# The hi and lo halves of the weights interleaved element by element in one tile: a decoder trunk on one core

## The chip, the cores and the metric

The kernel runs on one core of a Trainium2 chip. The metric is the device time of one execution in microseconds (us). A core has five engines that run beside each other, each with its own queue of instructions and held together by semaphores: TensorE (PE, with its weight loads as PEld), VectorE (DVE), ScalarE (ACT), GpSimdE (POOL) and SyncE (SP), which here issues the DMAs.

## What is computed

The reference is a decoder trunk over 512 tokens of width 1024 with two layers. The first mixes the tokens with a Mamba-2 SSD mixer, the second with differential attention with ALiBi; behind each stands a gated feed-forward net with a causal depthwise convolution of width 3. Every mixer is wrapped in an RMS norm before and one after it. All of it is float32, and most of the arithmetic is in eight matrix products with weights:

```python
proj = jnp.einsum('bsd,de->bse', u, w_in)          # SSD mixer, 1024 -> 6176
return jnp.einsum('bse,ed->bsd', y, w_out)         # 2048 -> 1024
h = jnp.einsum('bsd,df->bsf', u, w_up)             # net, 1024 -> 5632, twice
return jnp.einsum('bsf,fd->bsd', silu(gate) * up, w_down)   # 2816 -> 1024, twice
qkv = jnp.einsum('bsd,de->bse', u, w_qkv)          # attention, 1024 -> 3072
return jnp.einsum('bse,ed->bsd', out, w_out)       # 1024 -> 1024
```

## The kernel before

The activations lie transposed in SBUF, features over the 128 partitions and the 512 tokens along the free dimension, in chunks of 128 features. A product with a weight matrix is made in units: one unit is the weights of 128 output features for 8 chunks of input (1024 columns of 128x128 tiles, 512 KB) or, in the two down projections, for 11 chunks (1408 columns). There are 217 units in eight phases, in this order: MIX (49 units, the input projection of the SSD mixer, in a loop over 8 groups of 6 units with the scan's own matmuls between them), SOUT (16), UP0 (44), DN0 (16), QKV (24, in a loop over the heads with the attention between them), AOUT (8), UP1 (44), DN1 (16).

To keep float32 precision at the single-pass rate of the float32r type, every float32 operand is split into two float32r halves: hi, the rounded value, and lo, the rest. A tile product is then three matmuls: hi x hi and hi x lo with the hi half of the weights, and lo x hi with their lo half. That is `product` (lines 466 to 470): line 468 and 469 take the weights' hi half, line 470 their lo half. Each of the three is a matmul instruction with a weight load of its own, 128 columns in 128 partitions.

Of each unit SyncE loads the float32 weights into the tile `raw` (two slots, line 386). ScalarE copies them into the hi half (`split_hi`, line 416). VectorE subtracts hi from raw and writes the lo half (`split_lo_dve`, line 431); in the attention loop GpSimdE does that for 20 units (`split_lo`, line 422). TensorE then runs the unit. `w_hi` and `w_lo` have two slots each, so ScalarE may write a slot only when TensorE has finished the unit that was in it, two units back. To start a phase early there are further pairs of tiles: `own_hi`/`own_lo`, `fx_*`, `fy_*` for the feed-forward phases, and `ax_*`, `ay_*` for attention; `halves_of` (lines 322 to 333) names the pair of a unit. Hi and lo are two separate tiles in each case, and in each the elements of a unit are contiguous: the 128 weights of one load lie 4 bytes apart.

The moving operands are the activations, split in the same way (`hn_hi`/`hn_lo`, `y_*`, `h_*`, `o_*`), 512 tokens to a matmul in most cases. At the four boundaries between mixer and net the work goes by halves of the tokens, 256 columns to a matmul: the last pair of units of a phase (`pair_pe`, two pairs where the phase has two units to an output) and the first four units of the next one (`wide_start`), so that the norm of the first half of the tokens can run beside the products of the second.

The order on each engine is written out by hand. In VectorE's queue the split of a unit some places ahead stands between the steps of the convolution or of the attention (`ahead`), and ScalarE's splits stand between its activations. The waits around the change are: ScalarE waits in line 416 for the unit that frees its slot (`unit_done`) and for the DMA, VectorE in line 431 for hi (`hi_made`), TensorE at the head of a unit for lo (`lo_made`), and SyncE for lo too, before it loads over the raw slot.

Of the kernel before, what the change touches and what calls it, by code (L numbers as in the profile page):

```python
# [18 lines left out]
F32R = mybir.dt.float32r  # L19
# [4 lines left out]
P = 128  # L24
# [3 lines left out]
KC = D // P  # L28
# [9 lines left out]
UW = HU * P  # L38
# [65 lines left out]
def trunk(nc, x_in, w_mix, w_sout, w_up0, w_dn0, w_qkv, w_aout, w_up1, w_dn1, params, lam_in, out):  # L104
    ctx = ExitStack()
    with ctx:
        MIX, SOUT, UP0, DN0, QKV, AOUT, UP1, DN1 = PH = phases()
# [3 lines left out]
        def sb(name, shape, dt=F32, scope=ctx):  # L111
            return scope.enter_context(nc.sbuf_tensor(name, shape, dt))
# [4 lines left out]
        x = sb("x", [P, KC, S])  # L117
        raw = sb("raw", [P, 2, UW])
        sb("lead_in", [P, 56])
        w_hi = sb("w_hi", [P, 2, UW], F32R)  # L120
        w_lo = sb("w_lo", [P, 2, UW], F32R)
        sb("lead_out", [P, 72])
        par = sb("par", [P, NPAR])
        lam_v = sb("lam_v", [P, 4 * DH])
# [28 lines left out]
        with ExitStack() as ssm:  # L153
# [38 lines left out]
            ecs_bc = sb("ecs_bc", [P, HG, S], scope=ssm)  # L192
            sb("own_lead", [P, 112], scope=ssm)
            own_raw = sb("own_raw", [P, KC * P], scope=ssm)
            own_hi, own_lo = sb("own_hi", [P, KC * P], F32R, scope=ssm), sb("own_lo", [P, KC * P], F32R, scope=ssm)
        with ExitStack() as ffn:
            h_hi = sb("h_hi", [P, FC, S], F32R, scope=ffn)
            h_lo = sb("h_lo", [P, FC, S], F32R, scope=ffn)
            with ExitStack() as lap:
                ug_f = sb("ug_f", [P, FFN_T - 1 + S], scope=lap)  # L200
                cg = sb("cg", [P, S], scope=lap)
                cu = sb("cu", [P, S], scope=lap)
                sg = sb("sg", [P, S], scope=lap)
                hb = sb("hb", [P, S], scope=lap)
            fy_hi, fy_lo = sb("fy_hi", [P, 2, KC * P], F32R, scope=ffn), sb("fy_lo", [P, 2, KC * P], F32R, scope=ffn)
            fx_hi, fx_lo = sb("fx_hi", [P, 2, KC * P], F32R, scope=ffn), sb("fx_lo", [P, 2, KC * P], F32R, scope=ffn)
        with ExitStack() as att:
            o_hi = sb("o_hi", [P, NH, S], F32R, scope=att)
            o_lo = sb("o_lo", [P, NH, S], F32R, scope=att)
            qT = sb("qT", [P, 2, S], scope=att)  # L210
            kT = sb("kT", [P, 2, S], scope=att)
            vT = sb("vT", [P, 2, S], scope=att)
            vtok = sb("vtok", [P, 2, NB, P], scope=att)
            dist_i = sb("dist_i", [P, S], mybir.dt.int32, scope=att)
            dist = sb("dist", [P, S], scope=att)
            sc = sb("sc", [P, 2, 2, S], scope=att)
            pr = sb("pr", [P, 2, 2, S], scope=att)
            at = sb("at", [P, NB, S], scope=att)
            aT = sb("aT", [P, NB, S], scope=att)
            ob = sb("ob", [P, S], scope=att)  # L220
            on = sb("on", [P, S], scope=att)
            with ExitStack() as lap:
                osq = sb("osq", [P, S], scope=lap)
                nmx = sb("nmx", [P, 2, 2], scope=lap)
                den = sb("den", [P, 2, 2], scope=lap)
                cf = sb("cf", [P, 2, 2], scope=lap)
            ay_hi, ay_lo = sb("ay_hi", [P, 2, KC * P], F32R, scope=att), sb("ay_lo", [P, 2, KC * P], F32R, scope=att)
            ax_hi, ax_lo = sb("ax_hi", [P, 2, KC * P], F32R, scope=att), sb("ax_lo", [P, 2, KC * P], F32R, scope=att)

        bank = [ctx.enter_context(nc.psum_tensor(f"bank{i}", [P, S], F32)) for i in range(2)]  # L230
        b_norm = ctx.enter_context(nc.psum_tensor("b_norm", [P, S], F32))
# [84 lines left out]

        WIDE = (UP0, QKV, UP1)

        def slot_of(ph, j):
            return (ph.U0 + j) % 2  # L320

        def halves_of(ph, j, first=False):

            if first and ph in WIDE and j < 4:
                own = ((ax_hi, ax_lo), (ay_hi, ay_lo)) if ph is QKV else ((fx_hi, fx_lo), (fy_hi, fy_lo))
                hi, lo = own[j // 2]
                return hi[:, j % 2, :], lo[:, j % 2, :]
            if first and (ph is MIX and j == 2 or ph is SOUT and j == 6):
                return own_hi[:], own_lo[:]
            if first and ph is AOUT and j in (2, 3):  # L330
                return ax_hi[:, j - 2, 0:ph.width], ax_lo[:, j - 2, 0:ph.width]
            slot = slot_of(ph, j)
            return w_hi[:, slot, 0:ph.width], w_lo[:, slot, 0:ph.width]

        def acc_of(ph, j):
            return bank[(ph.Q0 + j) % 2]
# [14 lines left out]
        def raw_of(ph, j, first=False):  # L351
            if first and ph is MIX and j == 2:
                return own_raw[:]
            return first_raw[:, j, :] if first and ph in WIDE else raw[:, slot_of(ph, j), 0:ph.width]
# [108 lines left out]

        def product(acc, slot, c, hi, lo, first, last, weights=None):

            wh, wl = weights or (w_hi[:, slot, :], w_lo[:, slot, :])
            wh, wl = wh[:, c * P:(c + 1) * P], wl[:, c * P:(c + 1) * P]
            nc.tensor.matmul(acc[:], wh, hi, start=first, stop=False)  # L468
            nc.tensor.matmul(acc[:], wh, lo, start=False, stop=False)  # L469
            return nc.tensor.matmul(acc[:], wl, hi, start=False, stop=last)  # L470
# [1694 lines left out]
```

## Time and profile before

| | us |
|---|---|
| median of 3 runs | 1436.48 (1435.9 to 1438.88) |
| the profiled execution | 1436.27 |
| its span, from the first instruction to the last | 1434.5 |
| TensorE matmuls busy | 1417.3 (99%) |
| weight loads busy | 1192.6 (83%) |
| VectorE busy | 1027.8 (72%) |
| ScalarE busy | 621.3 (43%) |
| GpSimdE busy | 112.9 (8%) |

Busy times are unions of the recorded spans of an engine's instructions. Matmuls are pipelined and their recorded ends are modelled, so that neighbours overlap: the rate of the stream is the distance between two starts, not the recorded duration. In the timeline a row is start, duration, engine, line, operation, what is written and read, and the shapes; a row that merges several instructions ends with their count. L468 is line 468. "bank<-hn_hi,w_hi" is a matmul into the tile bank with hn_hi moving and w_hi as weights; 128x512 is the moving operand with its columns. PEclk is the TensorE clock that was granted, as a share of full speed.

### The profile page before, as it was taken

What the parts mean: (1) busy time and instruction counts of PE and PEld (TensorE: products, weight loads), DVE (VectorE), ACT (ScalarE), POOL (GpSimd) and SP (SyncE); (2) the same over time, 40 slices, a digit from 0 to 9 for tenths busy, and PEclk for the clock granted to TensorE, in tenths of its full rate; (3) what the DMA queues carried; (4) which work ended last, traced back from release to release, by engine and by line L of the source; (5) the groups of instructions that cost most, each with busy time, mean ns of one, the idle gap of its engine ahead of it and who ended that gap; (6) DMA issues with size and microseconds to landing.
All of it is one profiled execution on the core that took longest, in us unless ns stands there. A gap on an engine that the chain in (4) does not pass through costs nothing.

```text
span 1434.5 us, 21763 instructions
## 1 busy us (share of the span) xinstructions
PE 1417.3 (99%) x7506; PEld 1192.6 (83%) x7506; DVE 1027.8 (72%) x1575; ACT 621.3 (43%) x1019; POOL 112.9 (8%) x85
## 2 busy tenths in 40 slices
PE   8999999999999999999999999999999999999997
PEld 6888888888889888888888977777798888888887
DVE  6998889899437888888623677778588888886123
ACT  6656555557334323323323446556563332323221
POOL 0000000000110000000011032321110000000111
PEclk9999999999999999999999999999999999999999
DMA  4433332432231232323233112121212222233331
GB/s 169 176 137 126 142 125 109 138 140 74 89 132 38 96 102 88 102 91 110 101 101 139 31 59 74 59 74 56 89 63 84 92 102 96 94 105 103 101 101 60
DMA packets 37445, 142.34 MB, mean 99 GB/s; under 512 B 4176, under 2 KB 6352, under 8 KB 35344
## 3 DMA queue, kind: packets, MB, share of 16 engines
q1 hardware_dynamic: 37392, 141.63, 28.8%
q8 instruction: 34, 0.56, 0.2%
q14 instruction: 19, 0.16, 0.0%
HBM read 139.38 MB, written 2.23 MB: 99 GB/s over the span
## 4 chain that ended last, share of the span: by engine, by line
PE 94%; DVE 3%; DMA 1%; ACT 1%; issue 1%; SPq 0%; POOL 0%; POOLq 0%; ACTq 0%
PE bank L468 20%; PE bank L470 20%; PE bank L469 20%; PE b_x L468 7%; PE b_x L470 7%; PE b_x L469 7%; PE b_norm L1647 1%; PE b_norm L489 1%; PE b_y L1080 1%; PE b_y L468 1%; PE b_y L470 1%; PE b_y L469 1%; PE b_cb L1607 1%; DVE hn_lo L823 1%; PE b_x L1092 1%; PE b_y L1597 1%
## 5 line engine op out<-in xcount | busy, mean ns | idle before, releaser
L416 ACT ACTIVATE w_hi<-raw 128x1024 fp32r<-128x1024 f32 (+1 forms) x201 | 222.9, 1109 | 406.3 <-PE bank L470 291.1
L431 DVE TENSOR_TENSOR w_lo<-raw,w_hi 128x1024 fp32r<-128x1024 f32 (+1 forms) x181 | 234.1, 1293 | 229.2 <-ACT w_hi L416 229.1
L468 PE MATMUL bank<-hn_hi,w_hi 128*128 128x512 f32 x848 | 335.9, 396 | 2.9 <-DVE hn_lo L804 1.6
L470 PE MATMUL bank<-hn_hi,w_lo 128*128 128x512 f32 x848 | 330.8, 390 | 0.0
L469 PE MATMUL bank<-hn_lo,w_hi 128*128 128x512 f32 x848 | 330.3, 389 | 0.0
L468 PEld LDWEIGHTS bank<-hn_hi,w_hi 128*128 128x128 f32 x848 | 159.3, 188 | 38.1 <-DVE w_lo L431 3.2
L470 PEld LDWEIGHTS bank<-hn_hi,w_lo 128*128 128x128 f32 x848 | 159.2, 188 | 33.9
L469 PEld LDWEIGHTS bank<-hn_lo,w_hi 128*128 128x128 f32 x848 | 159.4, 188 | 32.1
L468 PE MATMUL bank<-h_hi,w_hi 128*128 128x512 f32 (+1 forms) x352 | 127.9, 363 | 0.0
L470 PE MATMUL bank<-h_hi,w_lo 128*128 128x512 f32 (+1 forms) x352 | 127.6, 362 | 0.0
L469 PE MATMUL bank<-h_lo,w_hi 128*128 128x512 f32 (+1 forms) x352 | 127.6, 362 | 0.0
L468 PE MATMUL b_x<-hn_hi,w_hi 128*128 128x512 f32 x320 | 124.6, 389 | 0.0
L469 PE MATMUL b_x<-hn_lo,w_hi 128*128 128x512 f32 x320 | 124.5, 389 | 0.0
L470 PE MATMUL b_x<-hn_hi,w_lo 128*128 128x512 f32 x320 | 124.5, 389 | 0.0
L1064 DVE SCALAR_TENSOR_TENSOR cv_s<-ug_s,par,cv_s 128x512 f32<-128x512 f32 x96 | 72.0, 750 | 6.9 <-DVE cv_s L1064 0.9
L469 PEld LDWEIGHTS bank<-h_lo,w_hi 128*128 128x128 f32 x352 | 66.4, 189 | 10.3
L470 PEld LDWEIGHTS bank<-h_hi,w_lo 128*128 128x128 f32 x352 | 66.4, 189 | 10.3
L468 PEld LDWEIGHTS bank<-h_hi,w_hi 128*128 128x128 f32 x352 | 66.4, 189 | 10.3
L1498 ACT ACTIVATE sg<-cg 128x512 f32<-128x512 f32 x44 | 27.9, 633 | 104.3 <-DVE cg L1064 104.3
L468 PEld LDWEIGHTS b_x<-hn_hi,w_hi 128*128 128x128 f32 x320 | 60.1, 188 | 13.0 <-issue 0.6
L469 PEld LDWEIGHTS b_x<-hn_lo,w_hi 128*128 128x128 f32 x320 | 60.1, 188 | 12.5
L470 PEld LDWEIGHTS b_x<-hn_hi,w_lo 128*128 128x128 f32 x320 | 60.1, 188 | 12.5
(326 smaller groups left out, 2476.7 us busy)
## 6 DMA issues: line engine op xcount, KB each, us to landing
raw<-w_up SPq DMA_DIRECT2D x80, 512.0 KB, 3.2
raw<-w_mix SPq DMA_DIRECT2D x48, 512.0 KB, 3.3
raw<-w_dn SPq DMA_DIRECT2D x32, 704.0 KB, 4.1
raw<-w_qkv SPq DMA_DIRECT2D x20, 512.0 KB, 3.2
acs_bc<-scratch SPq DMA_DIRECT2D x8, 1024.0 KB, 5.7
ecs_bc<-scratch SPq DMA_DIRECT2D x8, 1024.0 KB, 4.7
raw<-w_sout SPq DMA_DIRECT2D x16, 512.0 KB, 3.2
first_raw<-w_up SPq DMA_DIRECT2D x8, 512.0 KB, 6.4
```

The costliest lines, as they stand in the source:

```text
L416: nc.scalar.activation(halves_of(ph, j if own else rep, own or first and j < 4)[0], raw_of(ph, rep, first and j < 4), ACT.Copy).then_inc(h ...
L431: nc.vector.tensor_tensor(lo, raw_of(ph, rep, first), hi.bitcast(F32), ALU.subtract).then_inc(lo_made, 1)
L468: nc.tensor.matmul(acc[:], wh, hi, start=first, stop=False)
L469: nc.tensor.matmul(acc[:], wh, lo, start=False, stop=False)
L470: return nc.tensor.matmul(acc[:], wl, hi, start=False, stop=last)
L489: last = nc.tensor.matmul(b_norm[:, b:b + 1], squares[:, b * P:(b + 1) * P], mean_col[:, mean:mean + 1], start=True, stop=True)
L823: nc.vector.scalar_tensor_tensor(hn_lo[:, m, tokens(t)], x[:, m, tokens(t)], gain(*GAINS[b][1], m), hn_hi[:, m, tokens(t)].bitcast(F32), A ...
L1064: ins = nc.vector.scalar_tensor_tensor(dst, ug[:, t:t + S], col(wcol + t), dst, ALU.mult, ALU.add)
L1080: last = nc.tensor.matmul(dst, xdt[:, c, hh, :], m_t[:, hh, c * P:(c + 1) * P], start=True, stop=c == 0)
L1092: last = nc.tensor.matmul(b_x[:, c // 2, (c % 2) * 2 * P:(c % 2) * 2 * P + 2 * P], btok[:, c, :], xdd[:, c, :, :].rearrange("p h d -> p (h ...
L1498: nc.scalar.activation(sg[:], cg[:], ACT.Silu).then_inc(gate_ready, 1)
L1597: last = nc.tensor.matmul(scores_in[i % 2][:, t, 0:keys], qT[DH * t:DH * t + DH, b1, i * P:(i + 1) * P], kT[DH * t:DH * t + DH, b1, 0:keys ...
```

## The change

Each pair of tiles becomes one tile with a last dimension of 2, in which the two halves of one weight are neighbours: hi, lo, hi, lo. The new tile takes the place of the two old ones and has their size together, so the addresses of all other tiles stay as they are. `parts` gives the two views of it, with every second element. ScalarE writes hi, VectorE and GpSimdE read hi and write lo, and the weight loads of lines 468 to 470 read either half, each with a step of 8 bytes where it was 4. The raw tiles, the moving operands, the order of the instructions, and all waits are untouched.

```diff
-        w_hi = sb("w_hi", [P, 2, UW], F32R)
-        w_lo = sb("w_lo", [P, 2, UW], F32R)
+        w_both = sb("w_both", [P, 2, UW, 2], F32R)
...
-            own_hi, own_lo = sb("own_hi", [P, KC * P], F32R, scope=ssm), sb("own_lo", [P, KC * P], F32R, scope=ssm)
+            own_both = sb("own_both", [P, KC * P, 2], F32R, scope=ssm)
...
-            fy_hi, fy_lo = sb("fy_hi", [P, 2, KC * P], F32R, scope=ffn), sb("fy_lo", [P, 2, KC * P], F32R, scope=ffn)
-            fx_hi, fx_lo = sb("fx_hi", [P, 2, KC * P], F32R, scope=ffn), sb("fx_lo", [P, 2, KC * P], F32R, scope=ffn)
+            fy_both = sb("fy_both", [P, 2, KC * P, 2], F32R, scope=ffn)
+            fx_both = sb("fx_both", [P, 2, KC * P, 2], F32R, scope=ffn)
...
+        def parts(both):
+
+            return both[:, :, 0], both[:, :, 1]
+
...
             if first and ph in WIDE and j < 4:
-                own = ((ax_hi, ax_lo), (ay_hi, ay_lo)) if ph is QKV else ((fx_hi, fx_lo), (fy_hi, fy_lo))
-                hi, lo = own[j // 2]
-                return hi[:, j % 2, :], lo[:, j % 2, :]
+                own = (ax_both, ay_both) if ph is QKV else (fx_both, fy_both)
+                return parts(own[j // 2][:, j % 2, :, :])
             if first and (ph is MIX and j == 2 or ph is SOUT and j == 6):
-                return own_hi[:], own_lo[:]
+                return parts(own_both)
             if first and ph is AOUT and j in (2, 3):
-                return ax_hi[:, j - 2, 0:ph.width], ax_lo[:, j - 2, 0:ph.width]
+                return parts(ax_both[:, j - 2, 0:ph.width, :])
             slot = slot_of(ph, j)
-            return w_hi[:, slot, 0:ph.width], w_lo[:, slot, 0:ph.width]
+            return parts(w_both[:, slot, 0:ph.width, :])
...
-            wh, wl = weights or (w_hi[:, slot, :], w_lo[:, slot, :])
+            wh, wl = weights or parts(w_both[:, slot, :, :])
             wh, wl = wh[:, c * P:(c + 1) * P], wl[:, c * P:(c + 1) * P]
             nc.tensor.matmul(acc[:], wh, hi, start=first, stop=False)
```

The pairs `ax_*` and `ay_*` become `ax_both` and `ay_both` in the same way.

## Rows read from the trace of the kernel before

**Rows 1.** The page, part 1: busy time, share of the span, instructions.
```profile
PE 1417.3 (99%) x7506; PEld 1192.6 (83%) x7506; DVE 1027.8 (72%) x1575; ACT 621.3 (43%) x1019; POOL 112.9 (8%) x85
```

**Rows 2.** The page, part 4: the chain that ended last, by engine.
```profile
PE 94%; DVE 3%; DMA 1%; ACT 1%; issue 1%; SPq 0%; POOL 0%; POOLq 0%; ACTq 0%
```

**Rows 3.** Groups by form: busy us, mean ns of one, idle us before them.
```profile
L468 PE MATMUL bank<-hn_hi,w_hi 128*128 128x512 f32 x848 | 335.9, 396 | 2.9 <-DVE hn_lo L804 1.6 <-DVE w_lo L431 1.0 <-issue 0.2
...
L468 PE MATMUL bank<-h_hi,w_hi 128*128 128x256 f32 x88 | 25.2, 287 | 0.0
...
L468 PE MATMUL b_y<-hn_hi,fx_hi 128*128 128x256 f32 x64 | 18.7, 292 | 0.0
```

**Rows 4.** Timeline, down projection, 512 columns; lines 469 and 470 between.
```profile
701.19 0.39 PE L468 MATMUL bank<-h_hi,w_hi 128*128 128x512 f32 x1
...
701.87 0.39 PE L468 MATMUL bank<-h_hi,w_hi 128*128 128x512 f32 x1
```

**Rows 5.** Timeline, its last pair, 256 columns; lines 469 and 470 between.
```profile
1409.02 0.28 PE L468 MATMUL b_x<-h_hi,w_hi 128*128 128x256 f32 x1
...
1409.38 0.28 PE L468 MATMUL b_x<-h_hi,w_hi 128*128 128x256 f32 x1
```

**Rows 6.** Timeline, a norm's sums in the SSD loop: matmuls of one column.
```profile
128.88 0.95 PE L489 MATMUL b_norm<-mean_col,yt 128*128 128x1 f32 x8
128.88 0.86 PEld L489 LDWEIGHTS b_norm<-mean_col,yt 128*128 128x128 f32 x7
```

**Rows 7.** Timeline: four loads of one column of rcol, repeated 128 times.
```profile
1426.17 0.52 PEld L614 LDWEIGHTS b_cb<-ident,rcol 128*128 128x128 f32 x4 [0.64 <-DVE rcol L798]
```

**Rows 8.** Tile b_cb: duration ns min/median/max, first and last start us, form.
```profile
L558 PEld LDWEIGHTS b_cb<-ident x20: 192/333/338, 3.2 to 6.8; 128*128 128x128 f32 x20
...
L468 PEld LDWEIGHTS b_cb<-y_hi,w_hi x8: 187/188/188, 355.8 to 360.5; 128*128 128x128 f32 x8
```

**Rows 9.** Groups by form, the splits.
```profile
L431 DVE TENSOR_TENSOR w_lo<-raw,w_hi 128x1024 fp32r<-128x1024 f32 x149 | 182.0, 1222 | 85.1 <-ACT w_hi L416 85.1
L416 ACT ACTIVATE w_hi<-raw 128x1024 fp32r<-128x1024 f32 x169 | 178.7, 1057 | 266.0 <-PE bank L470 160.1 <-PE b_x L470 94.5 <-PE b_cb L470 7.8
...
L431 DVE TENSOR_TENSOR w_lo<-raw,w_hi 128x1408 fp32r<-128x1408 f32 x32 | 52.0, 1626 | 144.0 <-ACT w_hi L416 144.0
L422 POOL TENSOR_TENSOR w_lo<-raw,w_hi 128x1024 fp32r<-128x1024 f32 x20 | 48.3, 2417 | 107.7 <-ACT w_hi L416 107.7
L416 ACT ACTIVATE w_hi<-raw 128x1408 fp32r<-128x1408 f32 x32 | 44.2, 1381 | 140.3 <-PE bank L470 131.0 <-PE b_x L470 9.3
```

**Rows 10.** Windows (PE, PEld, DVE, ACT, POOL busy, PEclk): SSD group, up projection, attention.
```profile
94.28:135.44 41.16, 41.16 (x239) 34.61 (x237) 36.44 (x53) 23.22 (x38) 0.00 (x0) 1.00 0.37 128
...
522.00:544.00 22.00, 22.00 (x99) 18.22 (x98) 18.04 (x25) 6.79 (x9) 0.00 (x0) 1.00 0.30 95
...
889.81:914.45 24.64, 24.64 (x122) 18.71 (x122) 18.62 (x34) 14.14 (x30) 7.17 (x4) 1.00 0.20 65
```

**Rows 11.** Timeline, SSD loop: a lo half made, and its unit's first matmul.
```profile
126.98 1.22 DVE L431 TENSOR_TENSOR w_lo<-raw,w_hi 128x1024 fp32r<-128x1024 f32 x1
...
129.68 0.49 PE L468 MATMUL bank<-hn_hi,w_hi 128*128 128x512 f32 x1
```

**Rows 12.** Timelines of VectorE and ScalarE: down projection, then up projection.
```profile
731.43 1.62 DVE L431 TENSOR_TENSOR w_lo<-raw,w_hi 128x1408 fp32r<-128x1408 f32 x1 [5.91 <-ACT w_hi L416]
...
737.49 1.38 ACT L416 ACTIVATE w_hi<-raw 128x1408 fp32r<-128x1408 f32 x1 [6.10 <-PE bank L470]
...
544.79 1.23 DVE L431 TENSOR_TENSOR w_lo<-raw,w_hi 128x1024 fp32r<-128x1024 f32 x1 [0.72 <-ACT w_hi L416]
...
549.07 1.06 ACT L416 ACTIVATE w_hi<-raw 128x1024 fp32r<-128x1024 f32 x1 [4.32 <-PE b_x L470]
```

**Rows 13.** Line 468: its engine sat idle before it until (us, times).
```profile
  DVE w_lo L431: 5.4, 5
```

More of the change, by code:

```diff
@@ L226, in trunk @@
                 cf = sb("cf", [P, 2, 2], scope=lap)
-            ay_hi, ay_lo = sb("ay_hi", [P, 2, KC * P], F32R, scope=att), sb("ay_lo", [P, 2, KC * P], F32R, scope=att)
-            ax_hi, ax_lo = sb("ax_hi", [P, 2, KC * P], F32R, scope=att), sb("ax_lo", [P, 2, KC * P], F32R, scope=att)
+            ay_both = sb("ay_both", [P, 2, KC * P, 2], F32R, scope=att)
+            ax_both = sb("ax_both", [P, 2, KC * P, 2], F32R, scope=att)
         bank = [ctx.enter_context(nc.psum_tensor(f"bank{i}", [P, S], F32)) for i in range(2)]
```

## The prediction, made before the changed kernel ran

> **What bounds the kernel now.** I read the page first: the reader is to see there that the matmul row of TensorE fills 99% of the span and that its weight loads, the row below it, fill 83% beside it [rows 1]; and that the chain that ended last lies 94% on TensorE, 3% on VectorE [rows 2]. So the question is not how much work the change adds, but what TensorE's steady stream of loads and matmuls waits for. The profiled execution took 1436.27 us, its span is 1434.5 us; 1.8 us lie around the span. The median of the runs is 1436.48 us, 0.2 us more, so sums on the profiled execution can be read as sums on the median.
>
> The second view is the groups by form, for what the stream is made of. A unit of weights is split into hi and lo, and each 128x128 tile of it makes three matmuls (lines 468, 469, 470), each with a weight load of its own. From the loops: 217 units make 1832 tile products; where a boundary works in halves of the tokens a product is done twice with 256 columns instead of once with 512. Three opening phases (8 chunks x 4 units x 2 halves x 3 matmuls) are 576 of the narrow ones, the last pairs of the two down projections 528, of the SSD output 192, of the attention output 96: 1392 with 256 columns. The other 4800 have 512; [rows 3] has the largest groups of either kind.
>
> The third view is the timeline, for the distance from one start to the next, since a recorded matmul (0.39 us) overlaps the next. With 512 columns three steps take 701.87 - 701.19 = 0.68 us, 0.227 each [rows 4]; with 256 columns 1409.38 - 1409.02 = 0.36 us, 0.120 each [rows 5]. How fast loads can follow each other shows where the matmuls have one column: 7 loads in 0.86 us of which the last is 0.19, so (0.86 - 0.19) / 6 = 0.112 us a load [rows 6, 8]. So a load is hidden under a wide matmul with 0.115 us to spare, and under a narrow one with 0.008 us. The sum of the stream is 4800 x 0.227 + 1392 x 0.120 = 1090 + 167 = 1257 us, 88% of the span: only a change of these two distances, or a starving of the stream, moves the result by much.
>
> **The change, part by part.** Nothing is removed and nothing added: the same splits, loads, matmuls, waits and transfers, over the same bytes in total. Four readers or writers change their step from 4 to 8 bytes: the 5496 weight uses of the stream (6192 loads), ScalarE's write of hi, VectorE's (20 times GpSimdE's) read of hi, and their write of lo. The DMAs write only the raw tiles, which stay as they are, and what they wait for is only moved if the splits get longer.
>
> *Weight loads.* No row of before has a load with a step of 8 bytes, so I bound it. From below: 0 change. A gain is excluded as far as the load goes, for it is hidden already; the small excess of the distance (0.227 us where 512 columns at 2.4 GHz, the level that the granted 1.00 of [rows 10] means, are 0.213) might hide a collision of the two reads that another layout has less of, and I keep that as a case. Near the lower end stand two rows. The loads of one column repeated 128 times (a step of 0 bytes) follow each other at (0.52 - 0.19) / 3 = 0.110 us [rows 7], as the contiguous ones do, so the pattern by itself costs nothing. And the moving operand is read at 4 bytes per 0.227 / 512 = 0.44 ns, 9.0 bytes/ns in each partition, all through the kernel [rows 4]; the new load would pass over 8 bytes per 0.112 / 128 = 0.875 ns, 9.1 bytes/ns, the same pace of addresses, at half of the data. From above: half speed, 0.224 us, if half of each read is thrown away and the port is full now. The slowest loads of the trace, at its very start, are recorded with 333 ns against 188 to 192 [rows 8], 1.8 times, which is about that end. At 0.224 us the wide matmuls still hide it (0.227), the narrow ones don't: 1392 x (0.224 - 0.120) = 145 us. I take the lower end, 0: it is nearest to the pace of the moving operand. Between the ends the cost starts only at 0.120 us, 7% above now, and is then 1.4 us for each ns.
>
> The Trainium skill, Advanced Engine Details and Errata, section SBUF Cachelines, says that lines have 16 bytes and that an engine needs at least two hits on a line to absorb the memory's latency. Four-byte weights 8 bytes apart hit each line exactly twice, so by it the load stays at full speed, at the very edge. No row of before can confirm that edge. The skill's SBUF — State Buffer, section Door 1, adds that each access that crosses to a new line pays a penalty; the crossings double here (64 instead of 32 in a load), and read that way it speaks against the change: it is the first rival below.
>
> *The splits.* ScalarE takes 1057 ns for 1024 elements and 1381 for 1408, so (1381 - 1057) / 384 = 0.84 ns an element; VectorE 1222 and 1626, so 1.05 ns; GpSimdE 2417 ns for 1024 [rows 9]. With a step of 8 bytes they pass over 9.5 and 7.6 bytes/ns, again about the pace at which the moving operand is read. I take 0, with the doubling of the per-element part as the other end: +0.86 us and +1.07 us a unit of 1024. What hides part of it: in the SSD loop VectorE is busy 36.4 of 41.2 us for six units, in the up projection 18.0 of 22 for four, in attention 18.6 of 24.6 [rows 10]. In the SSD loop the lo half is ready at 126.98 + 1.22 = 128.20 and its first matmul starts at 129.68, 1.5 us later [rows 11]. In the down projection lo is ready at 731.43 + 1.62 = 733.05 and TensorE gives its old slot free, and so turns to the new unit, at 737.49, 4.4 us later; in the up projection 546.02 against 549.07, 3.0 us [rows 12]. So 0.5 us more per split would vanish everywhere in the steady loops. Bare are only the places where the stream waits for a split: 5.4 us in 5 waits in all [rows 13]. Once VectorE is late there, hn_lo, the taking of banks and the convolutions are queued behind it, and TensorE waits for those. With no change in duration all of this is 0.
>
> Sum: 0 + 0 + 0 on 1436.27, so I give the median, 1436.5 us. Its own range is 1432 to 1440, for the collision at the edge of the distances: 1 ns on 4800 + 1392 matmuls is already 6 us, and I expect under half of that.
>
> **The rivals.** *The load slows down at 8 bytes* (slower). For it: a load has only 0.008 us to spare in 1392 places; each line is left after two weights; nothing in the trace has this step. Against it: the moving read, at the same pace. Deciding point: 0.120 us a load. Two prices. A modest penalty, up to 0.140 us a load: 1392 x 0.020 = 28 us, 1464 us at most, middle 1450; chance 0.09. Half speed: 1436.5 + 145 = 1581 us; chance 0.11. In both, the whole loss lies in the stretches at the boundaries and none in the loops.
>
> *The splits slow down* (slower). For it: VectorE reads hi and writes lo within the same 8 bytes, and ScalarE writes beside weights that are being read. Against it: rows show no pace at which either is at its limit. At double time per element the up projection gets 2 x 1.07 us per pair of units where about 1 us of 10.9 is real slack (2.0 idle, 1.0 of it short waits for its own results), so 1.1 x 44 = 50 us; the SSD loop 6.4 us per group where 3.4 of the 4.8 idle are slack by the same account, 3.0 x 7 = 21; the bare waits 5 x 1.07 = 5: 1436.5 + 76 = 1512 us. VectorE becomes the bound there. It decides from 0.5 us a split. Chance 0.07.
>
> *The two reads of TensorE collide less* (faster). For it: 14 ns of each distance are unexplained. Against it: the distance is 13 to 14 ns above the columns' own time with 512 and 256 alike, like a fixed start cost. A gain of 2 ns on 6192 matmuls would be 12 us: 1424 us. Chance 0.03.
>
> That the change does not do what it says would be if the strided weights were copied first or loaded in pieces; no row has such a thing and its result would show as added instructions. It is inside the first rival.
>
> **How the numbers follow.** No change 0.70; load slower, modest 0.09, half speed 0.11; splits 0.07; faster 0.03. A measurement of this kernel tells about 0.2% (2.9 us) from no change. Faster is 0.03, slower 0.09 + 0.11 + 0.07 = 0.27, same 0.70. The likeliest time is 1436.5. For 8 times in 10 the range takes the first case (0.70) and the modest penalty to its end (0.09): 1432 to 1464; it leaves out 1512, 1581 and 1424, 0.21 together.
>
> **What would show it.** Right: the load recorded at 188 ns, starts 0.227 and 0.120 us apart, 0.112 us a load where the matmuls have one column (those are not strided, and are the yardstick within the same trace), splits at 1057, 1222 and 2417 ns. First rival: the 256-column starts further apart than 0.120 us while the 512-column ones stay at 0.227; above 0.227 both. Second: longer splits, idle TensorE with VectorE as its releaser in the SSD loop and up projection. The prediction is wrong if the pace of addresses is not what limits a read of weights: its one untested step is to carry the moving operand's pace over to the load.

## The result, and the profile of the changed kernel

The changed kernel takes 1467.01 us (median of 3 runs, 1465.41 to 1467.01) against 1436.48 us: the ratio is 1.0204, 95% interval 1.0181 to 1.0228, so it is slower by 30.5 us. The forecast was no change, 1436.5 us, and the range ended at 1464. The profiled execution took 1467.01 us, its span is 1465.2 us, 30.7 us more than before.

The page of the changed kernel, part 1 and the engines of the chain, against [rows 1] and [rows 2]:

```profile
PE 1449.2 (99%) x7506; PEld 1224.3 (84%) x7506; DVE 1029.2 (70%) x1575; ACT 638.5 (44%) x1019; POOL 113.3 (8%) x85
...
PE 95%; DVE 3%; DMA 1%; ACT 1%; issue 1%; SPq 0%; POOL 0%; POOLq 0%; ACTq 0%
```

The instructions are the same in number on every engine, and the chain is made of the same engines. So nothing was added and no new wait became the bound. The clock is not the cause either: the mean granted clock of the profiled execution was 0.998 before and is 0.999 now. TensorE is busy 32 us longer with the same 7506 matmuls. The groups by form, against [rows 3] and [rows 9] (lines stand two further down, 468 is 470 now):

```profile
L470 PE MATMUL bank<-hn_hi,w_both 128*128 128x512 f32 x848 | 340.6, 402 | 2.6 <-DVE hn_lo L806 1.2 <-DVE w_both L433 1.2 <-issue 0.2
...
L470 PE MATMUL bank<-h_hi,w_both 128*128 128x256 f32 x88 | 25.2, 287 | 0.0
...
L433 DVE TENSOR_TENSOR w_both<-raw,w_both 128x1024 fp32r<-128x1024 f32 x149 | 182.2, 1223 | 101.2 <-ACT w_both L418 101.1
L418 ACT ACTIVATE w_both<-raw 128x1024 fp32r<-128x1024 f32 x169 | 193.1, 1143 | 282.1 <-PE bank L472 172.7 <-PE b_x L472 98.5 <-PE b_cb L472 8.0
L470 PEld LDWEIGHTS bank<-hn_hi,w_both 128*128 128x128 f32 x848 | 164.8, 194 | 37.8 <-DVE w_both L433 3.1 <-issue 2.0 <-DVE vT L1752 0.4
...
L424 POOL TENSOR_TENSOR w_both<-raw,w_both 128x1024 fp32r<-128x1024 f32 x20 | 49.0, 2448 | 109.5 <-ACT w_both L418 109.5
```

The reader is to see four things. A wide matmul is recorded 6 ns longer (402 for 396 ns), a narrow one is not (287 and 287). The load beside it is recorded with 194 ns, where the prediction named 188 as the sign that it is unchanged. VectorE's split is unchanged (1223 ns, 1222 before); ScalarE's took 1143 ns for 1057, 8% more, GpSimdE's 2448 for 2417. And the splits wait longer for TensorE than they did (282.1 us before ScalarE's, 266.0 before [rows 9]): they are not what holds the kernel back.

The timeline gives the distances, as in [rows 4] and [rows 5]: six steps in the SSD loop, six in the up projection, three in the last pair of the down projection.

```profile
149.71 0.39 PE L470 MATMUL bank<-hn_hi,w_both 128*128 128x512 f32 x1
...
151.11 0.39 PE L470 MATMUL bank<-hn_hi,w_both 128*128 128x512 f32 x1
```

```profile
499.94 0.40 PE L472 MATMUL bank<-hn_hi,w_both 128*128 128x512 f32 x1
...
501.35 0.40 PE L472 MATMUL bank<-hn_hi,w_both 128*128 128x512 f32 x1
```

```profile
1438.32 0.28 PE L470 MATMUL b_x<-h_hi,w_both 128*128 128x256 f32 x1
...
1438.68 0.28 PE L470 MATMUL b_x<-h_hi,w_both 128*128 128x256 f32 x1
```

1.40 / 6 = 0.233 us and 1.41 / 6 = 0.235 us where 512 columns took 0.227, and 0.36 / 3 = 0.120 us for 256 columns, as before. Taken over all starts of the two traces, the 4720 wide matmuls that are followed without a wait stand 234.0 ns apart, before 227.2: 6.8 ns more, together 32 us. The waits inside the wide stream are about 1 us shorter in total, and the narrow matmuls and all the rest are 0.3 us shorter: 32 - 1 - 0.3 = 30.7 us, the whole loss. It is spread over the loops, and the boundaries pay nothing.

### The profile page after: what moved, and what is told of

It is laid out like the page before. It is cut to its first block, busy times and chain, and to the rows that moved or that the text cites. A ratio compares the mean times of both kernels' runs of the same rounds, so it can differ in the third digit from the quotient of the medians.

```text
span 1465.2 us, 21763 instructions
## 1 busy us (share of the span) xinstructions
PE 1449.2 (99%) x7506; PEld 1224.3 (84%) x7506; DVE 1029.2 (70%) x1575; ACT 638.5 (44%) x1019; POOL 113.3 (8%) x85
## 4 chain that ended last, share of the span: by engine, by line
PE 95%; DVE 3%; DMA 1%; ACT 1%; issue 1%; SPq 0%; POOL 0%; POOLq 0%; ACTq 0%
PE bank L470 21%; PE bank L471 20%; PE bank L472 20%; PE b_x L470 7%; PE b_x L471 7%; PE b_x L472 7%; PE b_norm L1649 1%; PE b_norm L491 1%; PE b_y L1082 1%; PE b_y L470 1%; PE b_y L471 1%; PE b_y L472 1%; PE b_cb L1609 1%; DVE hn_lo L825 1%; PE b_y L1599 1%; PE b_y L1085 1%
## 5 line engine op out<-in xcount | busy, mean ns | idle before, releaser
L418 ACT ACTIVATE w_both<-raw 128x1024 fp32r<-128x1024 f32 (+1 forms) x201 | 240.8, 1198 | 426.3 <-PE bank L472 307.0
L433 DVE TENSOR_TENSOR w_both<-raw,w_both 128x1024 fp32r<-128x1024 f32 (+1 forms) x181 | 234.2, 1294 | 252.3 <-ACT w_both L418 252.2
L470 PE MATMUL bank<-hn_hi,w_both 128*128 128x512 f32 x848 | 340.6, 402 | 2.6 <-DVE hn_lo L806 1.2
L472 PE MATMUL bank<-hn_hi,w_both 128*128 128x512 f32 x848 | 334.8, 395 | 0.0
L471 PE MATMUL bank<-hn_lo,w_both 128*128 128x512 f32 x848 | 334.7, 395 | 0.0
L470 PEld LDWEIGHTS bank<-hn_hi,w_both 128*128 128x128 f32 x848 | 164.8, 194 | 37.8 <-DVE w_both L433 3.1
L472 PEld LDWEIGHTS bank<-hn_hi,w_both 128*128 128x128 f32 x848 | 164.4, 194 | 34.1
L471 PEld LDWEIGHTS bank<-hn_lo,w_both 128*128 128x128 f32 x848 | 164.6, 194 | 31.6
L470 PE MATMUL bank<-h_hi,w_both 128*128 128x512 f32 (+1 forms) x352 | 129.9, 369 | 0.0
L472 PE MATMUL bank<-h_hi,w_both 128*128 128x512 f32 (+1 forms) x352 | 129.4, 368 | 0.0
L471 PE MATMUL bank<-h_lo,w_both 128*128 128x512 f32 (+1 forms) x352 | 129.2, 367 | 0.0
L470 PE MATMUL b_x<-hn_hi,w_both 128*128 128x512 f32 x320 | 127.0, 397 | 0.0
L472 PE MATMUL b_x<-hn_hi,w_both 128*128 128x512 f32 x320 | 126.7, 396 | 0.0
L472 PEld LDWEIGHTS bank<-h_hi,w_both 128*128 128x128 f32 x352 | 68.6, 195 | 10.9
L470 PEld LDWEIGHTS bank<-h_hi,w_both 128*128 128x128 f32 x352 | 68.8, 195 | 10.2
```

The lines of the kernel that those rows point to most:

```text
L418: nc.scalar.activation(halves_of(ph, j if own else rep, own or first and j < 4)[0], raw_of(ph, rep, first and j < 4), ACT.Copy).then_inc(h ...
L433: nc.vector.tensor_tensor(lo, raw_of(ph, rep, first), hi.bitcast(F32), ALU.subtract).then_inc(lo_made, 1)
```

## The experiments

Each kernel is the one before with one edit, timed beside it, or a small kernel that measures the cost by itself.

**One tile, no step.** hi and lo share a tile, but 128 columns of hi and 128 of lo in turn: every place of the change, and all reads and writes stay contiguous.

```diff
-        w_hi = sb("w_hi", [P, 2, UW], F32R)
-        w_lo = sb("w_lo", [P, 2, UW], F32R)
+        w_both = sb("w_both", [P, 2, HU, 2, P], F32R)
...
+            return both[:, :, 0, :], both[:, :, 1, :]
```

> Hi and lo share one tile as in the changed kernel, but in blocks of 128 elements instead of element by element: every load and every split has its step of 4 bytes again, only the place is that of the changed kernel. Theory A (the 8-byte step of the weight loads costs each 512-column matmul 6.5 ns): 1436.5 us, 512-column starts 0.227 us apart, ScalarE's split 1057 ns. Theory B (the 8-byte step of the splits' writes does it): 1436.5 us too. Theory C (it is the place of the halves in one tile, the step does nothing): 1467 us and 0.233 us.

Measured: 1435.72 us against 1435.52, ratio 1.0001 (0.9992 to 1.0011).

```profile
L470 PE MATMUL bank<-hn_hi,w_both 128*128 128x512 f32 x848 | 335.8, 396 | 2.0 <-DVE hn_lo L806 0.9 <-DVE w_both L433 0.8 <-issue 0.3
...
L418 ACT ACTIVATE w_both<-raw 128x1024 fp32r<-128x1024 f32 x169 | 178.7, 1057 | 265.0 <-PE bank L472 159.6 <-PE b_x L472 94.5 <-PE b_cb L472 7.8
```

396 and 1057 ns are the values of [rows 3] and [rows 9]. The shared tile, its place and its traffic cost nothing.

**Only the loads have the step.** hi and lo stay two tiles and the splits stay contiguous; the weights themselves are laid out in memory so that two 128-column tiles of a unit alternate element by element (the eleventh of a down unit stays as it is).

```diff
+            return slice(at * P + c % STEP, at * P + c % STEP + (P - 1) * STEP + 1, STEP)
...
-            wh, wl = wh[:, c * P:(c + 1) * P], wl[:, c * P:(c + 1) * P]
+            wh, wl = wh[:, columns(c, wh.shape[1] // P)], wl[:, columns(c, wh.shape[1] // P)]
```

> Hi and lo in two tiles as before and all splits contiguous, but each pair of 128x128 weight tiles lies interleaved in them (the weights come so from memory), so that every load has a step of 8 bytes (of 11 tiles in the down projections the last one stays contiguous). Theory A (load step): 1467 us less a little for the last tiles (1465 to 1467), 0.233 us between 512-column starts, 0.120 with 256 columns, and ScalarE's split back at 1057 ns. Theories B (split step) and C (place): 1436.5 us and 0.227.

Measured: 1463.33 us against 1435.52, ratio 1.0203 (1.0186 to 1.0220).

```profile
L476 PE MATMUL bank<-hn_hi,w_hi 128*128 128x512 f32 x848 | 340.1, 401 | 2.6 <-DVE hn_lo L812 1.2 <-DVE w_lo L432 1.2 <-issue 0.2
...
L417 ACT ACTIVATE w_hi<-raw 128x1024 fp32r<-128x1024 f32 x169 | 178.6, 1057 | 289.5 <-PE bank L478 177.9 <-PE b_x L478 100.3 <-PE b_cb L478 8.1
```

Three steps of its wide stream in the SSD loop:

```profile
150.01 0.39 PE L476 MATMUL bank<-hn_hi,w_hi 128*128 128x512 f32 x1
...
150.71 0.39 PE L476 MATMUL bank<-hn_hi,w_hi 128*128 128x512 f32 x1
```

The splits are those of before (1057 ns) and 27.8 of the 30.5 us are there by the medians; the two ratios, 1.0203 here and 1.0204 for the change, cannot be told apart. The distance is (150.71 - 150.01) / 3 = 0.233 us; over the whole trace wide starts stand 233.3 ns apart, narrow ones 119.9 ns. So the step of the weight loads is the cause.

**Only the splits have the step.** The writes of hi and lo and the read of hi go in steps of 8 bytes, and the weights are laid out so that the tiles then hold the same as before.

```diff
+        def every_second(t):
+            return t.rearrange("p (k s) -> p s k", s=2)
...
-            nc.vector.tensor_tensor(lo, raw_of(ph, rep, first), hi.bitcast(F32),
+            nc.vector.tensor_tensor(every_second(lo), raw_halves(raw_of(ph, rep, first)), every_second(hi.bitcast(F32)),
```

> The reverse: all loads contiguous in two tiles, but ScalarE, VectorE and GpSimdE write hi and lo with a step of 8 bytes (first the even, then the odd elements; the raw weights come in that order). Theory A: 1436.5 us, 0.227 us, though ScalarE's split may stay at 1143 ns, since it is hidden. Theory B: 1467 us and 0.233 us. Theory C: 1436.5 us.

Measured: 1435.94 us against 1435.52, ratio 1.0006 (0.9997 to 1.0016).

```profile
L422 ACT ACTIVATE w_hi<-raw 128x1024 fp32r<-128x1024 f32 x169 | 192.9, 1141 | 257.9 <-PE bank L476 154.9 <-PE b_x L476 91.8 <-PE b_cb L476 7.6
L437 DVE TENSOR_TENSOR w_lo<-raw,w_hi 128x1024 fp32r<-128x1024 f32 x149 | 182.2, 1223 | 86.2 <-ACT w_hi L422 86.1
```

ScalarE's 84 ns more are real (1141 ns), they come from its own step, and they are hidden: the slack that the prediction read for the splits was there.

**The price of a step by itself.** A kernel of stages with 48 matmuls each, the loads of one stage at one step (elements 1, 2, 4, 8 apart and more), the matmuls 512, 384, 256, 128 or 2 columns wide; then two stages in which the moving operand has a step of 8 bytes; then copies of 1024 elements by ScalarE and differences by VectorE and GpSimdE, one at a time. It leaves out the whole model.

```diff
+        def w_of(i, step):
+            at = i // step % groups * P * step + i % step
+            return wts[:, at:at + (P - 1) * step + 1:step]
...
+                last = nc.tensor.matmul(acc[0][:, 0:512], w_of(i, 2), move[:, i % 8, 0:512], start=i == 0, stop=i == 47)
```

> A kernel of its own that computes nothing of the model: stretches of 48 matmuls, each with its own weight load, for 512, 384, 256, 128 and 2 columns and loads with steps of 4, 8, 16 and 32 bytes (12, 64 and 128 too at 512 columns); then ScalarE, VectorE and GpSimdE splits of 1024 elements with steps of 4, 8 and 16 bytes while TensorE stands still. Theory A: 0.227 us a matmul at 512 columns and 4 bytes, 0.233 at 8 bytes; at 256 columns 0.120 for both; with 384 columns either +6.5 ns (a fixed loss per load, which 256 columns hide under the load's own pace) or +4.9 ns (a loss per column). If the load itself is slower at 8 bytes, it shows with 2 columns as more than 0.112 us. With 16 bytes, one weight to a line of 16 bytes, I expect the load at half speed, 0.22 us, and so 0.22 or more with 2 to 384 columns. Theories B and C: 0.227 at every step. ScalarE: 1057 and 1143 ns for steps of 4 and 8 bytes if its slowing is its own, 1057 for both if it came from TensorE's reads beside it.

Its timeline: start, length of the stage, line. 148, 151, 154: 512 columns with steps of 4, 8, 16 bytes; 181, 184, 187, 190: 256 columns with 4, 8, 16, 32 bytes; 193, 196, 199, 202: 128 columns with these; 217, 220: moving operand at 8 bytes, with contiguous loads and with loads at 8 bytes.

```profile
27.70 11.05 PE L148 MATMUL acc<-move,wts 128*128 128x512 f32 x48
...
38.59 11.36 PE L151 MATMUL acc<-move,wts 128*128 128x512 f32 x48
...
49.79 11.45 PE L154 MATMUL acc<-move,wts 128*128 128x512 f32 x48
...
146.47 5.92 PE L181 MATMUL acc<-move,wts 128*128 128x256 f32 x48
...
152.24 5.91 PE L184 MATMUL acc<-move,wts 128*128 128x256 f32 x48
...
157.98 11.37 PE L187 MATMUL acc<-move,wts 128*128 128x256 f32 x48
...
169.19 11.72 PE L190 MATMUL acc<-move,wts 128*128 128x256 f32 x48
...
180.75 5.47 PE L193 MATMUL acc<-move,wts 128*128 128x128 f32 x48
...
186.06 5.82 PE L196 MATMUL acc<-move,wts 128*128 128x128 f32 x48
...
191.71 11.41 PE L199 MATMUL acc<-move,wts 128*128 128x128 f32 x48
...
202.92 11.72 PE L202 MATMUL acc<-move,wts 128*128 128x128 f32 x48
...
257.47 22.00 PE L217 MATMUL acc<-move,wts 128*128 128x512 f32 x48
...
279.30 21.94 PE L220 MATMUL acc<-move,wts 128*128 128x512 f32 x48
```

The difference of two starts, over 48, is the distance. With 128 columns the load sets it: (186.06 - 180.75) / 48 = 0.111 us at 4 bytes, (191.71 - 186.06) / 48 = 0.118 at 8, (202.92 - 191.71) / 48 = 0.234 at 16, and at 32 hardly more (a stage of 11.72 us for 11.41). With 256 columns it is 0.120 and 0.120 us, (169.19 - 157.98) / 48 = 0.234 at 16 bytes and (180.75 - 169.19) / 48 = 0.241 at 32. The granted clock was 1.00 from the stage of line 148 to that of line 196, and 0.68 and 0.50 in those of lines 199 and 202; as the 256-column stages give the same distances at 1.00, these two loads do not hang on it. With 512 columns, under which either load has 0.11 us to spare, it is (38.59 - 27.70) / 48 = 0.227 and (49.79 - 38.59) / 48 = 0.233 us. That is the change, in a kernel that has nothing but loads and matmuls. The moving operand at 8 bytes takes (279.30 - 257.47) / 48 = 0.455 us (granted clock 0.93), and 0.453 from start to start within line 220 (granted 1.00): half speed.

Two parts of the expectation got another answer. With 384 columns the step costs nothing (0.174 us contiguous, 0.173 at 8 bytes, lines 169 and 172), where both a fixed loss per load and a loss per column were to show one. And the stages with 2 columns, which were to measure the load alone, ran at a granted clock of 0.50: 0.213 us at 4 and at 8 bytes, which says nothing of the load at 1.00. The stages with 128 columns stand in for them.

ScalarE's copies, TensorE idle, at 4, 8 and 16 bytes, and VectorE's differences at the same steps:

```profile
301.27 1.06 ACT L55 ACTIVATE dst<-x 128x1024 fp32r<-128x1024 f32 x1 [281.81 <-PE acc L220]
...
305.62 1.12 ACT L63 ACTIVATE dst<-x 128x1024 fp32r<-128x1024 f32 x1
...
316.55 2.00 ACT L79 ACTIVATE dst<-x 128x1024 fp32r<-128x1024 f32 x1
```

```profile
332.99 1.23 DVE L100 TENSOR_TENSOR dst<-x,dst 128x1024 fp32r<-128x1024 f32 x1 [332.99 <-ACT dst L93]
...
338.03 1.23 DVE L108 TENSOR_TENSOR dst<-x,dst 128x1024 fp32r<-128x1024 f32 x1
...
343.07 2.00 DVE L116 TENSOR_TENSOR dst<-x,dst 128x1024 fp32r<-128x1024 f32 x1
```

ScalarE pays most of its 8% at 8 bytes without any neighbour (1.12 for 1.06 us), VectorE nothing (1.23 at either).

**Four apart instead of two.** The second experiment with four tiles interleaved, loads at 16 bytes.

```diff
-STEP = 2
+STEP = 4
```

> As e2_load_step, but four weight tiles interleaved: every load has a step of 16 bytes (of 11 tiles the last three stay contiguous), splits contiguous. From the stretches of m1_loads: 0.235 us with 512 columns, 0.2335 with 256. 4800 x 8.1 ns = 39 us and 1392 x 113.5 ns = 158 us, less the contiguous tiles of the down projections (3 of 11: 144 of 528 narrow, about 16 us, and 216 wide, 2 us): 1436.5 + 179 = 1615 us. If the loads of a real stream are slowed further by the engines that write beside them, more than 1640.

Measured: 1623.99 us in one run, the kernel before beside it 1434.88. Summed over all starts, the wide stream is 44 us longer (10 us of it are waits) and the narrow one 141 us: 170.7 to 311.2 us for 1392 matmuls, whose starts were 0.222 us apart on average. That is 9 us above the expected 1615, which had no waits in it. The narrow part is the rival of half speed as the prediction priced it (145 us, at the boundaries); the 44 us in the wide stream the prediction did not have. So it was right as a price of the narrow matmuls and wrong as a threshold: it lies at one weight to 16 bytes, and the change has two.

**By width.** If the loss were in the load, it would show at the narrow end; if it were per column, it would grow with the width. More stages of the same kind, with other widths, with bases shifted, and with fewer weights in a load.

```diff
+                last = nc.tensor.matmul(acc[1][:, 0:508], w_of(i, 1), move[:, i % 8, 0:508], start=i == 0, stop=i == 47)
...
+                last = nc.tensor.matmul(acc[1][:, 0:512], wts[:, i % 60 * 128 + 1:i % 60 * 128 + 129], move[:, i % 8, 0:512], start=i == 0, stop=i == 47)
```

> A kernel of its own that computes nothing of the model, stretches of 48 matmuls with their loads as before. All distances measured so far at full clock lie on a grid of 6.67 ns (16 columns): 34 steps at 512 columns with contiguous weights, 35 with a step of 8 bytes, 26 at 384 and 18 at 256 for both. Theory D: the slower load (0.118 us a load instead of 0.111 where the matmul has 128 columns) pushes something over an edge of that grid, at certain widths only; between 384 and 512 columns the loss is then 0 or one whole step of 6.67 ns, by width, and depends on the bases of weights and moving operand. Theory E: the loss comes from the columns themselves beyond some width; it then grows from 0 at 384 to 6.5 ns at 512 in small parts. Theory F: it is the odd base of every second tile (4 bytes off 8) and not the step: then even bases alone give 0.227 us with a step of 8 bytes, and a contiguous load with its base 4 bytes off gives 0.233. With fewer weights in a load (96, 64, 32) theory D says the loss is gone (0.227), since the load ends earlier; theories E and F keep it.

Lines 135 and 138: 508 columns at 4 and 8 bytes; 141 and 144: 512 columns at 4 and 8; 153: 512 columns, contiguous, but every load begins 4 bytes later; 156: 8 bytes later.

```profile
209.72 11.10 PE L135 MATMUL acc<-move,wts 128*128 128x508 f32 x48
220.65 11.05 PE L138 MATMUL acc<-move,wts 128*128 128x508 f32 x48
231.54 11.07 PE L141 MATMUL acc<-move,wts 128*128 128x512 f32 x48
242.44 11.36 PE L144 MATMUL acc<-move,wts 128*128 128x512 f32 x48
...
276.04 11.32 PE L153 MATMUL acc<-move,wts 128*128 128x512 f32 x48
287.20 11.24 PE L156 MATMUL acc<-move,wts 128*128 128x512 f32 x48
```

At 508 columns the distance is (220.65 - 209.72) / 48 = 0.2277 us contiguous and (231.54 - 220.65) / 48 = 0.2269 at 8 bytes: no loss. At 512 it is 0.2271 and 0.2333. So theory E, a loss that grows with the columns, fell. A contiguous load that begins 4 bytes later takes (287.20 - 276.04) / 48 = 0.2325 us. That half of theory F held; the other fell: with a step of 8 bytes, even bases alone and odd ones alone take 0.233 us alike (lines 147 and 150). Theory D said that fewer weights in a load would take the loss away, and that fell too: with 96, 64 and 32 of them the contiguous load itself took 0.230 to 0.232 us. A shift of the moving operand does it as well: with contiguous weights and the moving operand 4, 8, 12 and 16 bytes later the distance is 0.236, 0.233, 0.230 and 0.231 us (lines 168, 174, 180, 186), so it is not only a matter of a base off 16 bytes. So 0.227 at 512 columns is not the plain case, to which the step adds something; it is a best case, and several things break it.

**A shifted base in the real kernel.** That can be tried without any step: the kernel before, its w_hi beginning 4 bytes later, its w_lo 20 bytes later, which is 4 bytes past a multiple of 16 too.

```diff
-        w_hi = sb("w_hi", [P, 2, UW], F32R)
-        w_lo = sb("w_lo", [P, 2, UW], F32R)
-        sb("lead_out", [P, 72])
+        w_hi = sb("w_hi", [P, 2 * UW + 4], F32R)[:, 1:1 + 2 * UW].rearrange("p (s w) -> p s w", s=2)
+        w_lo = sb("w_lo", [P, 2 * UW + 4], F32R)[:, 1:1 + 2 * UW].rearrange("p (s w) -> p s w", s=2)
+        sb("lead_out", [P, 64])
```

> The kernel before with one thing changed: the tiles w_hi and w_lo begin one element (4 bytes) later in memory. All loads stay contiguous, nothing is interleaved, all splits stay contiguous too. Theory D (the distance at 512 columns depends on how the reads of the load fall beside those of the moving operand, not on the step as such): the stretches of m2_widths gave 0.2324 us instead of 0.2267 for such a base, so 4704 wide loads from these tiles x 5.7 ns = 27 us, 1463 us. Theory A in its first form (only a step of 8 bytes costs): 1436 us.

Measured: 1459.28 us against 1436.85, ratio 1.0156 (1.0139 to 1.0172).

```profile
L468 PE MATMUL bank<-hn_hi,w_hi 128*128 128x512 f32 x848 | 338.3, 399 | 2.2 <-DVE w_lo L431 1.2 <-DVE hn_lo L804 0.8 <-issue 0.3
...
L468 PEld LDWEIGHTS bank<-hn_hi,w_hi 128*128 128x128 f32 x848 | 159.4, 188 | 43.0 <-DVE w_lo L431 2.6 <-issue 2.0 <-DVE vT L1750 0.5
```

The loads are recorded with the same 188 ns as before and the wide matmuls pay all the same: 232.9 ns from start to start in the mean, 5.7 ns more. In the last small kernel a load with such a base follows the next at 0.112 us, a plain one at 0.111 (lines 78 and 75). So the loss doesn't need a slower load.

The tiles own_hi and own_lo were not moved, and they serve as a check within the same trace: 18 steps with the moved w_hi and w_lo, then 18 with own_hi and own_lo, both in the bank b_cb with y_hi and y_lo moving.

```profile
361.07 0.39 PE L468 MATMUL b_cb<-y_hi,w_hi 128*128 128x512 f32 x1
...
365.27 0.39 PE L468 MATMUL b_cb<-y_hi,w_hi 128*128 128x512 f32 x1
...
388.21 0.39 PE L468 MATMUL b_cb<-y_hi,own_hi 128*128 128x512 f32 x1
...
392.30 0.39 PE L468 MATMUL b_cb<-y_hi,own_hi 128*128 128x512 f32 x1
```

(365.27 - 361.07) / 18 = 0.233 us with the moved tiles, (392.30 - 388.21) / 18 = 0.227 with the unmoved ones. So the loss hangs on where the loads' words lie. The total, 22.4 us, is less than the 27 us expected: the wide stream is 25.5 us longer, and the narrow one 2.5 us shorter, for narrow matmuls with the moved tiles start 116.8 ns apart (119.9 before) and with the unmoved fx and fy 119.8 as before. The same shift that costs the wide ones helps the narrow ones.

**Where the best case ends.** A last kernel of 60 matmuls a stage goes through more widths and bases and takes the kernel's own order (hi, hi, lo).

```diff
+                last = nc.tensor.matmul(acc[0][:, 0:510], w_of(i, 2), move[:, i % 8, 0:510], start=i == 0, stop=i == 59)
...
+                last = nc.tensor.matmul(acc[0][:, 0:512], wts[:, i // 3 % 30 * 256 + i % 3 // 2:i // 3 % 30 * 256 + i % 3 // 2 + 255:2], move[:, i // 3 % 4 + 4 * (i % 3 == 1), :], start=i == 0, stop=i == 59)
```

> A kernel of its own that computes nothing of the model, stretches of 60 matmuls with their loads: at 128 and 192 columns, where the load sets the pace, contiguous loads with bases 0, 4, 8 and 12 bytes off and steps of 8 and 12 bytes; then 18 widths from 256 to 510 columns with steps of 4 and 8 bytes; then 512 columns again, also in the kernel's order (hi, hi, lo of the same tile) interleaved and in two tiles. Theory D: the load alone is a little slower at 8 bytes (0.118 against 0.111 us) and perhaps with a shifted base, while the distance of wide matmuls is columns / 2.4 GHz + 13.3 ns at best and up to 20 ns, by width, for either step; the step of 8 bytes loses at 512 because 512 is a best width for contiguous loads. Theory G (a load of 8-byte step always takes 6.7 ns from a matmul that is wide enough): every width above 400 is slower by 6.7 ns at 8 bytes. The kernel's order: 0.2267 in two tiles, 0.2333 to 0.2356 interleaved, for the two patterns that the changed kernel's trace shows.

Lines 213 and 216: 510 columns at 4 and 8 bytes; 219 and 222: 512 at 8 and 4; 234: the changed kernel's three loads in turn; 237: those of the kernel before.

```profile
498.07 13.80 PE L213 MATMUL acc<-move,wts 128*128 128x510 f32 x60
511.71 14.16 PE L216 MATMUL acc<-move,wts 128*128 128x510 f32 x60
525.71 14.16 PE L219 MATMUL acc<-move,wts 128*128 128x512 f32 x60
539.70 13.77 PE L222 MATMUL acc<-move,wts 128*128 128x512 f32 x60
...
595.07 14.15 PE L234 MATMUL acc<-move,wts 128*128 128x512 f32 x60
609.05 13.77 PE L237 MATMUL acc<-move,wts 128*128 128x512 f32 x60
```

The changed order takes (609.05 - 595.07) / 60 = 0.233 us, the old one, by the lengths of the two stages, (14.15 - 13.77) / 60 = 0.006 us less. Over the widths no simple rule holds (distances in ns from start to start within a stage; 496 from the kernel before this one):

```
columns      256    320    384    432    456    488    496    500    506    510    512
step 4 B     120.3  146.5  173.4  195.8  209.0  225.5  220.1  223.6  226.9  227.3  226.7
step 8 B     119.9  146.7  173.3  193.4  204.4  220.0  225.3  226.6  226.7  233.3  233.3
```

The step loses at 496, 500, 510 and 512 columns and wins at 432, 456 and 488. Most of the values lie on or near multiples of 6.67 ns (18, 22, 26, 29, 33, 34, 35 of them), which is the time of 16 columns at 2.4 GHz, the level of the granted 1.00. Theory G, that every matmul above 400 columns pays, fell with it. Theory D held in so far as the loss goes by width, but its "13.3 ns at best" above the columns' own time fell as well: with 304 columns it is 137.8 - 126.7 = 11 ns, contiguous (line 123).

## Why the prediction was wrong, step by step

*What bounds the kernel* held: the result is the number of wide matmuls times the growth of their distance, and nothing else.

*"Between the ends the cost starts only at 0.120 us a load"* is the step that failed. The load did grow, from 0.111 to 0.118 us, within its 0.008 us to spare under a narrow matmul, and the narrow ones paid nothing, as that step says. But it also says that a wide matmul hides a load up to 0.227 us for free. It doesn't: 4720 of them paid 6.8 ns each, 32 us, with half of the time to spare. Work that is hidden beside a stream was taken for work that can't touch it. The term belongs per wide matmul, not per ns above a threshold.

The prediction did name the place where this could hide, "a collision of the two reads", but only as a gain and as a few us of width (1 ns on each matmul, "under half of that" expected). What spoke for more stood in its rows: a distance 13.6 ns above the columns' own 213 at 512 and 13.3 above 107 at 256. It read that as "a fixed start cost". The runs show that it is none: at 488 columns the contiguous stage has 225.5 - 203.3 = 22 ns, at 512 it has 13, and a 4-byte shift of the weights makes that 19.

*The choice of 0 for the load, by the pace of the addresses*, fell as an argument though the load lost only 6%. Its premise was that a read at 8 bytes per step costs what one at 4 does if it passes over the same bytes in the same time. The load at 0.118 us passes at 8.7 bytes/ns, just under the moving operand's 9.0, which fits; and the moving operand at 8 bytes takes 0.453 to 0.455 us, the same 9.0 bytes/ns again, and at 16 bytes the load takes 0.234 us, 8.8. So a limit near 9 bytes/ns describes these rows, and by it the load's 6% would be its first touch of that limit. It is not one of addresses as such: at 32 bytes the load takes 0.240 us, hardly more than at 16. Each new stretch of 16 bytes costs about 1.8 ns, whether two weights or one are taken from it (0.118 / 64 and 0.234 / 128). The argument chose the right end for the load, and the loss was then where it did not look. The 333 ns of [rows 8], taken there as about the end of half speed, are no measure of a read that is slow by its layout: in the small kernel contiguous loads are recorded with 333 ns as well, in the stage that ran at a granted clock of 0.50 (line 205).

The Trainium skill, Advanced Engine Details and Errata, section SBUF Cachelines, asks for at least two hits on a line of 16 bytes. VectorE bears it out (1.23 us at 4 and 8 bytes, 2.00 at 16), the load and ScalarE nearly (0.111, 0.118, 0.234 us; 1.06, 1.12, 2.00), the moving operand of TensorE does not: it has two hits at 8 bytes and runs at half speed (0.455 us). The Trainium skill, TensorE: Matmul & The Clock Gate, section Step-by-step: what each phase is for, says that the load has a read port of its own and takes no bandwidth from the running matmul. No run here shows the ports. But that a hidden load leaves the running matmuls alone, as one might conclude, does not hold here: with the shifted base it is the same load, recorded with the same 188 ns, and 5.7 ns more a matmul.

*The splits* were right. VectorE 1223 ns; ScalarE 8% longer, far from the doubling that was the other end, and hidden, 1.0006 by itself.

*The rivals.* The first had the direction and the cause (the load at 8 bytes) but the wrong place: "in both, the whole loss lies in the stretches at the boundaries and none in the loops" is the exact reverse of the trace. That its modest case ended at 1464 us is a coincidence. Its half-speed case came true one step further, at 16 bytes. The second needed 0.5 us more per split; the largest growth was 0.11 us (the 1408 columns of ScalarE, 1489 for 1381 ns). The third, a gain from fewer collisions, looked in the right place, the excess of each distance over the columns' own time, with the wrong sign; whether that excess is a collision of the two reads no run shows.

*What stays open.* Why the loads and the moving reads fall into these patterns: the runs show that step, base and width matter, not how. And the last 3 us between the second experiment and the changed kernel (30.5 against 27.8). The eleventh tiles, 72 wide matmuls that keep their old layout there and start 229.4 ns apart, are 0.3 us of it. The rest is one stretch: in the first up and down projection (some 490 to 790 us of the span, the second timeline above) the changed kernel's wide starts are 235.6 ns apart in the mean, elsewhere 233.4; 1270 matmuls by 2.2 ns are 2.8 us. The layout alone doesn't make it, for the second up and down projection run the same code on the same tiles at 233.3 ns, and the small kernel in the same order shows 233.1. It may come and go from one execution to the next: of the second experiment's four runs three took 1463.2 to 1463.4 us and one 1467.47, of the changed kernel's three two took 1467.01 and one 1465.41. Only one execution of each was traced, so this is not shown.

## What to carry to other kernels

Where a stream of matmuls is the bound, the layout of its weights is a cost of its own even if their load is hidden twice over: measure the distance from start to start in a small kernel at the real width, base and step, before the layout is chosen. For these float32r matmuls a step of two elements in weights is cheap but not free at 512 columns (and free at 256 and 384), a step of four costs the load half of its speed, and a step in the moving operand costs that from two on. A loss of a few ns shows in no wait and no idle time, only in the distances of a timeline, times their count.

## What the runs showed of the hardware that was not expected

- A contiguous weight load that begins 4 bytes later slows the 512-column matmuls beside it from 227.2 to 232.9 ns and speeds the 256-column ones from 119.9 to 116.8 ns, together 22 us of this kernel, while the load's own duration stays at 188 ns.
- With weights and moving operand at their own bases, 512-column matmuls are 34 (contiguous) or 35 (8 bytes) times 6.67 ns apart; with a shifted base of either, 228 to 236 ns. 508 columns are not faster than 512 (0.2277 us contiguous).
- A moving fp32r operand with a step of 8 bytes runs at half speed (0.453 us for 512 columns), a weight load with the same step at 94% (0.118 for 0.111 us).
- ScalarE's write at 8 bytes costs 6% alone and 8% in the kernel; VectorE's costs nothing; at 16 bytes both take 2.00 us for 1024 elements.
